# Chunked attention taken two heads at a time, with the g_b projection between its pieces

## What is computed

```python
proj = h @ w_in[l]
xr, yr, q, k, v, g_a, g_b = jnp.split(proj, IN_SPLITS, axis=-1)
hr = rg_lru(causal_depthwise_conv(xr, ...), ...)
y_a = (jax.nn.gelu(yr) * hr) @ w_up_a[l]
qh = rms_norm(q.reshape(B, S, N_HEADS, HEAD_DIM), q_gain[l])
kh = rms_norm(k.reshape(B, S, N_HEADS, HEAD_DIM), k_gain[l])
y_b = chunked_attention(qh, kh, vh, rel_table[l]) @ w_up_b[l]
gates = jnp.concatenate([g_a, g_b], axis=-1) + gate_bias[l]
x = x + (sigmoid(gates_a) * y_a + sigmoid(gates_b) * y_b) @ w_out[l]
```

## Time and profile before

| | |
|---|---|
| time, median of 3 runs | 2779.78 us (2779.47 to 2781.95) |
| profiled execution, own time | 2780.0 us |
| its span, first to last instruction | 2778.2 us |
| granted TensorE clock, mean | 0.996 |
| TensorE busy | 2734.7 us, 98% |
| weight loads busy | 2196.4 us, 79% |
| DVE, ACT, POOL busy | 833.2, 1188.3, 1179.1 us |
| attention of the first layer, first transposes to the second half of w_up_b | 857.36 to 951.27 us |

### The profile page before, as it was taken

How to read it: one execution, slowest core, us unless ns; L and a number is a source line. 1 busy time by engine, 2 the same in 40 slices (tenths; PEclk the granted TensorE clock), 3 DMA queues, 4 the chain that set the end, 5 groups by cost and what they waited for, 6 DMA issues and landing times.

```text
span 2778.2 us, 35532 instructions
## 1 busy us (share of the span) xinstructions
PE 2734.7 (98%) x11968; PEld 2196.4 (79%) x11968; DVE 833.2 (30%) x1515; ACT 1188.3 (43%) x1680; POOL 1179.1 (42%) x524
## 2 busy tenths in 40 slices
PE   7999999999999999999999999999999999999998
PEld 6888878878776688888888888788787757888887
DVE  4222035630015432221132211448100164322212
ACT  5443235742445534443243432457324364444422
POOL 3444444445442234444444444344453423444444
PEclk9999999999999999999999999999999999999999
DMA  7333223332331233332333323332333212333322
GB/s 259 99 91 102 94 85 97 91 100 84 98 98 41 71 91 99 98 98 91 100 99 98 92 91 99 87 93 84 110 96 97 72 40 88 95 91 99 98 92 91
DMA packets 247056, 263.82 MB, mean 95 GB/s; under 512 B 9040, under 2 KB 233072, under 8 KB 246928
## 3 DMA queue, kind: packets, MB, share of 16 engines
q1 hardware_dynamic: 242768, 253.70, 30.6%
q10 hardware_dynamic: 4160, 8.47, 0.9%
HBM read 259.95 MB, written 10.57 MB: 97 GB/s over the span
## 4 chain that ended last, share of the span: by engine, by line
issue 40%; PE 40%; POOL 18%; DVE 1%; POOLq 1%; ACT 0%; DMA 0%; DVEq 0%; ACTq 0%
POOL wlo L414 18%; PE ps L1095 10%; PE ps L1100 10%; PE ps L1099 10%; PE ps L1295 2%; PE ps L1223 2%; PE ps L1277 1%; PE ps L1208 1%; PE ps L1244 1%; PE ps L1239 1%; PE ps L1243 1%; POOLq L421 0%; POOLq L413 0%; PE ps L1325 0%; DVE p L1013 0%
## 5 line engine op out<-in xcount | busy, mean ns | idle before, releaser
L414 POOL TENSOR_TENSOR wlo<-raw,whi 128x1024 fp32r<-128x1024 f32 x475 | 1140.7, 2408 | 1464.1 <-ACT whi L463 1463.7
L1095 PE MATMUL ps<-h_lo,whi 128*128 128x512 f32 x2400 | 945.9, 394 | 21.8 <-DVE h_lo L748 9.8
L1100 PE MATMUL ps<-h_hi,wlo 128*128 128x512 f32 x2400 | 936.5, 390 | 0.0
L1099 PE MATMUL ps<-h_hi,whi 128*128 128x512 f32 x2400 | 936.4, 390 | 0.0
L463 ACT ACTIVATE whi<-raw 128x1024 fp32r<-128x1024 f32 x475 | 500.2, 1056 | 737.3 <-PE ps L1095 676.4
L1095 PEld LDWEIGHTS ps<-h_lo,whi 128*128 128x128 f32 x2400 | 452.0, 188 | 126.9 <-DVE h_lo L748 14.9
L1099 PEld LDWEIGHTS ps<-h_hi,whi 128*128 128x128 f32 x2400 | 452.4, 188 | 96.6 <-issue 3.8
L1100 PEld LDWEIGHTS ps<-h_hi,wlo 128*128 128x128 f32 x2400 | 452.0, 188 | 94.9
L1095 PE MATMUL ps<-act_lo,whi 128*128 128x512 f32 x704 | 273.9, 389 | 0.0
L1099 PE MATMUL ps<-act_hi,whi 128*128 128x512 f32 x704 | 273.9, 389 | 0.0
L1100 PE MATMUL ps<-act_hi,wlo 128*128 128x512 f32 x704 | 273.9, 389 | 0.0
(11 more groups left out here) (139 smaller groups left out, 2635.6 us busy)
## 6 DMA issues: line engine op xcount, KB each, us to landing
raw<-in_w_in SPq DMA_DIRECT2D x124, 512.0 KB, 3.7
raw<-in_w_gate SPq DMA_DIRECT2D x88, 512.0 KB, 3.7
raw<-in_w_up SPq DMA_DIRECT2D x88, 512.0 KB, 3.7
raw<-in_w_down SPq DMA_DIRECT2D x80, 512.0 KB, 3.4
raw<-in_w_up_b SPq DMA_DIRECT2D x19, 512.0 KB, 3.6
rel_band<-rel_rows ACTq DMA_DIRECT2D x1, 8192.0 KB, 39.7
raw<-in_w_out SPq DMA_DIRECT2D x16, 512.0 KB, 3.4
raw<-in_rg_band SPq DMA_DIRECT2D x14, 512.0 KB, 3.5
```

Of the source, the lines that this page charges most:

```text
L414: nc.gpsimd.tensor_tensor(wlo[:, s, :], raw[:, s, :], whi[:, s, :].bitcast(F32), ALU.subtract).then_inc(lo_made, 1)
L1095: ins = pe.matmul(ps[:, b, :], w_hi, x_lo, start=start, stop=False)
L1099: pe.matmul(ps[:, b, :], w_hi, x_hi, start=False, stop=False)
L1100: return pe.matmul(ps[:, b, :], w_lo, x_hi, start=False, stop=stop)
```

## The change

Attention is written for two heads, 2t and 2t+1, at once.

- **Scores**: the product of head e (0 or 1) reads its own 64 partitions of q and k, without a padded copy; the two heads' products alternate and go to different banks (0, 1 and 2, 3). POOL's copies into `square` are gone. The four blocks of queries are taken as LATE (512 and 384 keys) and EARLY (256 and 128 keys).
- **Output**: the products with v of the two heads alternate, one into the lower and one into the upper half of bank 6.
- **g_b** leaves its place ahead of w_up_a. Its 8 tiles are computed one per pair of heads, in bank 7, from chunks of 128 columns by all 1024 rows, and their products stand between the pieces of attention: 3, 3, 9 and 9 of the 24. DVE copies the tile out raw; ACT takes the sigmoid later, in the w_up_b stage.
- **Transposes** go through banks 4 and 5, one for each head, three times a pair; ACT copies all of them (three per head). Half of `pt` of the odd head lies in `square`.
- **DVE** does `normalised` for both heads in two parts, LATE and EARLY, with the copy of g_b between. TensorE waits for both parts before the next pair's transposes.
- **Bias**: three places instead of two; SP waits for the exponentials of a pair, fetches two heads' bias (four DMAs) and then issues the next chunk's load.
- **After the last pair**: attention's output is `o_hi`, `o_lo`, apart from `h_hi`, `h_lo`, which g_b still needs. The first half of w_up_b follows the last pair instead of standing beside the last two heads.
- **v stage**: the first pair's scores stand after v's fifth and sixth chunk of eight; before, two heads' scores stood after the sixth and seventh.

```diff
-TURNED = [(4, 0, KS * P, (0,)), (5, KS * P, KS * P, (1, 3)), (7, 2 * KS * P, 2 * P, (2,))]
+TURNED = [(0, KS * P, (0,)), (KS * P, KS * P, (1, 3)), (2 * KS * P, 2 * P, (2,))]
+LATE, EARLY = (3, 2), (1, 0)
+BANDS_HELD = 3
+        def score_bank(e, i):
+            return 2 * e + i % 2
+        TURN_BANK, OUT_BANK, GB_BANK = (4, 5), 6, 7
...
@@ sync
+                for t in range(KD + 1):
+                    if t < KD:
+                        load(win[:, bass.ds(l * KD, KD), G0 + (KD + t) * P:G0 + (KD + t + 1) * P], (KD, P))
+                    else:
+                        load(up_b[:, bass.ds(l * KD, 4), 0:PAIR], (4, PAIR))
+                    if t >= 2:
+                        sp.wait_ge(exp_made, C.next(exp_made, 2 * KS))
+                        for head in range(BANDS_HELD + 2 * (t - 2), min(BANDS_HELD + 2 * (t - 1), HEADS)):
+                            band_of(head)
...
@@ gpsimd
-                    nc.gpsimd.tensor_tensor(square[p_:p_ + HD, head % 2, :], q[p_:p_ + HD, head // 2, :], zeros,
-                                            ALU.add).then_inc(q_placed, C.made(q_placed))
...
+                for t in range(KD):
+                    ring(AHEAD + t)
...
@@ scalar
+                for t in range(KD):
+                    for parts in zip(*pt):
+                        for e, part in enumerate(parts):
+                            act.wait_ge(turned[e], C.next(turned[e]))
+                            nc.scalar.activation(part, ps[:, TURN_BANK[e], 0:part.shape[1]], ACT.Copy
+                                                 ).then_inc(bank_read[TURN_BANK[e]], C.made(bank_read[TURN_BANK[e]]))
+                    ring()
+                    if t + 1 < KD:
+                        exps(LATE)
+                        exps(EARLY)
+                    act.wait_ge(heads_out, C.next(heads_out))
+                    nc.scalar.activation(o_hi[:, t, :], ps[:, OUT_BANK, :], ACT.Copy
...
@@ tensor
+                    for i in blocks:
+                        for e in range(2):
+                            head = slice(e * HD, (e + 1) * HD)
+                            pe.matmul(ps[:, score_bank(e, i), 0:(i + 1) * P], q[head, t, i * P:(i + 1) * P],
+                                      k[head, t, 0:(i + 1) * P], start=True, stop=True
+                                      ).then_inc(scored, C.made(scored))
...
+                for t in range(KD):
+                    gb_slot = chunk()
+                    pe.wait_ge(bank_read[GB_BANK], C.now(bank_read[GB_BANK]))
+                    pe.wait_ge(late_prob, C.next(late_prob, 2 * len(LATE)))
+                    pe.wait_ge(early_prob, C.next(early_prob, 2 * len(EARLY)))
+                    turn(0)
+                    gate_b([0])
+                    turn(1)
+                    gate_b([1])
+                    turn(2)
+                    if t + 1 < KD:
+                        scores(t + 1, LATE)
+                    gate_b([2, 3, 4])
+                    if t + 1 < KD:
+                        scores(t + 1, EARLY)
+                    gate_b([5, 6, 7])
+                    weighted(t)
```

More of the change, by code:

```diff
@@ L644, in _ @@
                         ring()
-                for t in range(2 * KD):
+                for t in range(KD):
                     if t % 2 == 0 and t:
                         ring(2)
-                    read(mix_bank(G_T + t), ya_out[:, t, :] if t < KD else gb_out[:, t - KD, :], ACT.Sigmoid,
-                         bias=col("gate", t))
+                    read(mix_bank(G_T + t), ya_out[:, t, :], ACT.Sigmoid, bias=col("gate", t))
                 for j in range(KD // 2):
@@ L688, in _ @@
                     C.step(bank_read[b])
-                def exps(head):
-                    for i in range(KS):
-                        C.step(bank_read[i])
-                        act.wait_ge(bank_read[i], C.now(bank_read[i]))
-                        part = prob[head % 2][:, tri(i):tri(i + 1)]
-                        nc.scalar.activation(part, part, ACT.Exp, scale=-1.0, bias=mx[:, head % 2, i:i + 1],
-                                             accum_out=total[:, head % 2, i:i + 1]
-                                             ).then_inc(exp_made, C.made(exp_made))
@@ L1252, in _ @@
                             head_sums(2 * KD - 2)
+                        if (half, a) == (1, 0):
+                            pe.wait_ge(qk_made, C.next(qk_made, 2 * KD))
+                            scores(0, LATE)
                         if (half, a) == (1, 2):
-                            pe.wait_ge(qk_made, C.next(qk_made, 2 * KD))
-                            scores(0)
-                        if (half, a) == (1, 4):
-                            scores(1)
+                            scores(0, EARLY)
@@ new lines, in weighted @@
+                def weighted(t):
+                    for b in (*TURN_BANK, OUT_BANK):
+                        pe.wait_ge(bank_read[b], C.now(bank_read[b]))
+                    for g, (_, _, keys) in enumerate(TURNED):
+                        at = 0
+                        for j in keys:
+                            for e in range(2):
+                                head = 2 * t + e
+                                ins = pe.matmul(ps[e * HD:(e + 1) * HD, OUT_BANK, j * P:S],
+                                                v[:, j, head * HD:(head + 1) * HD], pt[e][g][:, at:at + (KS - j) * P],
+                                                start=j == 0, stop=j == TURNED[-1][2][-1])
+                            at += (KS - j) * P
+                    ins.then_inc(heads_out, C.made(heads_out))
+                    C.step(bank_read[OUT_BANK])
@@ L1264, in up_b_begun @@
+                s = chunk()
+                for m in range(2):
                     b = mix_bank(UB_T + m)
```

312 lines of the change are left out of this document (157 added, 155 removed).

## The result

| | before | after |
|---|---|---|
| time, median of 4 runs each | 2780.81 us (2779.47 to 2781.95) | 2720.85 us (2717.46 to 2721.22) |
| ratio | | 0.978, 95% interval 0.9766 to 0.9794 |
| profiled execution, own time | 2780.0 us | 2717.46 us |
| its span | 2778.2 us | 2715.6 us |
| granted TensorE clock, mean | 0.996 | 0.997 |

The change makes the kernel 2.2% faster, 60 us. The forecast was 2730 us in a range from 2704 to 2768: the sign and the range held, the gain came out 10 us larger.

What follows compares the result with a forecast made beforehand. TensorE was taken as the bound. A layer went from 143.4 to 118.4 us (pairs of 14.0, the last 10.6), a gain of 25.0, 50 us for two layers: 2780 - 50 = 2730 us, range 2704 to 2768.

Steps and rivals of the forecast that it cites:

- the overlap: Scores and output of a pair: two heads' products partly overlap, staggered, taking 2.81 and 2.70 us, each 4.32 before; 54%.
- Nothing overlaps: Rival for scores and output: they stay at 4.32 us each a pair, the gain is 0, 2780 us; 10%.
- only one kind: Rival: just one of scores and output overlaps, 12 to 13 us come back in each layer, 2755 us; 10%.
- six passages: TensorE moving between whole and half array, in and out of LATE, EARLY and output: 0.15 us each, 0.9 a pair.
- wholly side by side: Rival: the two heads' products overlap completely, scores and output 2.16 us each a pair, 2711 us; 8%.
- The wait for v's last copy: End of the v stage: the first transposes wait 1.0 us for v's last copy and the handoffs.
- DVE's margin of 0.6 us: From the first EARLY score, DVE needs 5.6 us and TensorE 6.2, so TensorE stays the bound.
- DVE and POOL don't collide: Rival: POOL's `wlo` slips onto DVE's division, 22 us, 2752; 10% together with other chains giving back 10 to 30 us.
- The ring of the chunk load: Slower rival: late-landing g_b chunks hold up ACT's rounding and exponentials; at 10 us landing 18.0 us a pair, 2786; 8%.

Runs made afterwards that it cites:

- both in one half: The changed kernel with both heads' scores read from the lower 64 rows and both outputs put into the lower 64 columns: 2787.96 us, ratio 1.0023.
- Products written apart: The changed kernel with all products with v of the even head ahead of all of the odd head's: 2744.96 us, ratio 0.9868.
- the kernel before with half rows: The kernel before with scores over the head's own 64 rows of q and k, without POOL's padded copies: 2789.34 us, ratio 1.0026.
- The copy made twice: The changed kernel with DVE's copy of g_b's tile made twice ahead of the EARLY division: 2727.0 us, ratio 0.9806.

## Why the forecast was right, and where it was off

**The bound and the mechanism held.** TensorE sets the pace, half-filled products of two heads run at once, and without that (both in one half) there is no gain: 67.1 us of overlap carry a change that would otherwise lose 5.7. The range held the result in spite of a wrong step in the overlap, which was put too small. "Nothing overlaps" and "only one kind" were real cases with nearly the right prices: 2788 measured for 2780 forecast, and 2754.4 and 2754.6 for 2755.

**The term that was mis-sized is the overlap.** Of a pair's 14.0 us:

| | forecast | measured | |
|---|---|---|---|
| scores | 2.81 | 2.16 | 2560 column-passes for two heads at 0.844 ns |
| output | 2.70 | 2.16 | the same |
| six passages | 0.9 | 1.04 | 0.19 in LATE's 1.70, 0.21 in EARLY's 0.86, 0.17 in the output's 2.33, 0.24 and 0.23 in the nine products of g_b behind each of the scores |
| transposes, g_b | 7.58 | 7.84 | 2.21 transposes; 0.09 and 0.10 more in each three products of g_b between them |
| sum | 14.0 | 13.2 | |

The failed step is "Instructions go in order, and a head's second pass needs its first pass out of the same half. So the run is A1, then A2 beside B1". It isn't so: in the rows of after first pass starts with first pass and second with second. Products written apart showed why: TensorE doesn't hold the other half's pass back behind passes written ahead of it that haven't begun, three of them in that run. The rival that the case belonged to, wholly side by side, had 8% and 2711 us. Its mechanism is the one that happened; its time was missed by 10: 6 since the passages and the places where g_b meets the transposes cost 0.4 us a pair more than counted, 1 by the wait for v's copy, and 3 by which the median lies over the profiled execution. The Trainium skill, "TensorE: Matmul & The Clock Gate", Part 3, has products in different tiles start a few ns apart, and the rows agree (0.00 us). The same part has products start and end strictly in program order, and loads run beside products only when the row group differs. The measurements decide against both here: the odd head's pass at 841.36 starts ahead of three that are written before it, and the output, whose halves share their rows, overlaps wholly (2.33 for 4.45), with the odd head's weight load at 823.28 beside the even head's product.

**The passages** were estimated at 0.15 us and are 0.17; the one more change in the kernel before with half rows cost 0.19 (2.35 for 2.16). The places where g_b meets the transposes, whole array on both sides, had been costed at nothing and are 0.26 us a pair.

**The wait for v's last copy** ahead of the first transposes was named rightly (row at 812.41), and was 1.47 us, not 1.0.

**DVE's margin of 0.6 us** wasn't there. DVE took 5.4 us of the 5.6 reckoned; but TensorE needs 0.86 + 2.27 + 2.33 = 5.46 for what was put at 6.2, again since the overlap is complete. The copy made twice shows what a slower DVE would have cost: of 0.6 us more, 0.58 came through in every pair.

**DVE and POOL don't collide.** One pair's rows in after:

```profile
844.35 0.69 DVE L1030 CUSTOM_DVE_ANT_0 p<-ps,tmp 128x512 f32<-128x512 f32 x1
```

```profile
844.37 2.41 POOL L436 TENSOR_TENSOR wlo<-raw,whi 128x1024 fp32r<-128x1024 f32 x1 [10.17 <-ACT whi L476]
```

`wlo` runs 5.6 to 8.0 us into this pair (forecast 5.8 to 8.2), beside bias and not beside the division, which starts at 848.62. In the first layer's other pairs it starts 5.3 to 6.2 us in and is over at least 1.2 us ahead of the division.

**The ring of the chunk load** isn't closed. ACT waits 0.18 us for its data in this pair and at most 0.81 in the first layer, in the shadow of TensorE's work:

```profile
843.23 1.06 ACT L476 ACTIVATE whi<-raw 128x1024 fp32r<-128x1024 f32 x1 [0.18 <-DMA raw<-in_w_in]
```

One figure of that rival doesn't come out of its own sum: a landing of 9.1 us gives 17.1 us a pair, 3.1 x 14 = 44 us back; all of the 50 us is gone at 9.5.

**For a layer** the forecast's 118.4 us came out as 112.5: 7 x 0.8 us for the pairs, 0.4 for the last (10.17 for 10.6), 0.5 for the scores in the v stage with their passages (2.9 for 3.4), less 0.47 for v's copy and 0.13 for the first half of w_up_b (5.57 for 5.44). Two layers give 11.8, and 2730 lay 12.5 over the profiled 2717.46.

## What to carry to other kernels

Two float32 products that each fill half the rows or half the columns of the array, placed in opposite halves and written alternately, take the time of one, here 2.16 us for 4.32; a product that fills half takes as long as a full one, so half-filling alone wins nothing and costs about 0.2 us at each change between whole and half array. Where so much is gained on TensorE, count again, with the overlap complete, how long each other engine has: here DVE, reckoned with 0.6 us to spare, ended level. Where independent products stand between dependent pieces matters as much: in one piece at the end they cost 72 us, more than the whole gain, in part by the waits that they no longer cover and in part since they release a chunk late for ScalarE.

## What was not expected of the hardware

- TensorE starts a pass in a free half of the array ahead of three passes for the busy half that are written before it and haven't begun (841.36 against 841.47), and not ahead of four or more: two heads' LATE scores take 1.71 us with four passes in a row, as when alternating (1.70), while outputs with eight in a row take 3.86 against 2.33.
- Column halves overlap as fully as row halves: putting both heads in one half costs 2.12 us a pair for the output and 2.15 for the scores.
- In the kernel with g_b in one piece the granted clock fell to 0.90 over 815 to 832 us, where TensorE was busy 13.57 of 17 us, and stayed at 1.00 over 883 to 900, where it was busy 13.10 of 17. In the first it was 0.66 over 820 to 825 us, a mean of the two levels, 1.2 and 2.4 GHz. What tells the two stretches apart wasn't settled.
